# A third normalisation applied after the gate's products instead of before them

## The reference, cut to what matters

```
x = x + mixed @ w_out
x = x + _hier_moe(_rmsnorm(x, ln2), w_rg, b_rg, w_re, b_re, w1, w3, w2)
x = x + jax.nn.sigmoid(_rmsnorm(x, ln3) @ w_ple_gate) * (p @ w_ple_proj)
```

```
def _rmsnorm(x, g):
    y = xf * lax.rsqrt(jnp.mean(xf * xf, axis=-1, keepdims=True) + EPS)
    return (y * g.astype(jnp.float32)).astype(x.dtype)
```

## Time and profile before

| | us |
|---|---|
| median of 3 runs | 1957.49 |
| lowest and highest | 1956.63, 1961.32 |
| the profiled execution, its own time | 1956.76 |
| its span | 1955.0 |
| PE busy | 1816.6 |
| DVE, ACT, POOL busy | 1154.0, 880.4, 118.4 |

### The profile page before, as it was taken

The page is one execution under the profiler, slowest core; times in us unless marked ns, Lnnn a source line. Parts: engine busy times, 40 slices in busy tenths (PEclk is TensorE's granted clock), DMA queues, the critical chain, the costliest instruction groups (busy, mean ns, idle before and its releaser), DMA issues.

```text
span 1955.0 us, 23219 instructions
## 1 busy us (share of the span) xinstructions
PE 1816.6 (93%) x9628; PEld 1526.7 (78%) x9628; DVE 1154.0 (59%) x1373; ACT 880.4 (45%) x982; POOL 118.4 (6%) x75
## 2 busy tenths in 40 slices
PE   5999889747999999999999899999999999996998
PEld 3899768746877778997897777887887788884898
DVE  4985547897862222323442536886886788885533
ACT  3333355344443435321223235775665666663322
POOL 0100004231320010000000000000000000000000
PEclk9999889878999999999999579999999999999999
DMA  7443433322454354473555237997998899995540
GB/s 221 130 130 99 124 86 89 84 86 65 122 173 140 135 175 147 123 276 120 169 151 169 70 119 241 362 367 257 341 341 290 293 335 342 350 320 148 148 114 27
DMA packets 385912, 365.51 MB, mean 187 GB/s; under 512 B 18388, under 2 KB 361476, under 8 KB 383688
## 3 DMA queue, kind: packets, MB, share of 16 engines
q1 hardware_dynamic: 381704, 345.07, 56.7%
q0 software_dynamic: 4096, 18.88, 2.7%
HBM read 353.19 MB, written 10.72 MB: 186 GB/s over the span
## 4 chain that ended last, share of the span: by engine, by line
PE 83%; DVE 11%; ACT 3%; issue 2%; DMA 1%; POOL 0%; DVEq 0%; SPq 0%; ACTq 0%
PE psum L1577 22%; PE psum L770 18%; PE psum L783 9%; PE psum L1564 7%; PE psum L844 6%; PE psum L732 4%; PE psum L1742 2%; PE psum L1505 2%; PE psum L753 2%; PE psum L1764 1%; PE psum L616 1%; PE psum L1739 1%; PE psum L837 1%; DVE weights_low L2095 1%; DVE arena L2239 1%
## 5 line engine op out<-in xcount | busy, mean ns | idle before, releaser
L1001 DVE TENSOR_TENSOR weights_low<-arena,weights_high 128x2048 fp32r<-128x2048 f32 x192 | 439.7, 2292 | 103.1 <-ACT weights_high L870 102.9
L1577 PE MATMUL psum<-input_high,weights_high 128*128 128x320 f32 x1264 | 406.7, 322 | 47.9 <-ACT arena L1886 25.5
L870 ACT ACTIVATE weights_high<-arena 128x2048 fp32r<-128x2048 f32 x192 | 367.6, 1915 | 108.1 <-PE psum L783 58.3
L1577 PE MATMUL psum<-input_low,weights_high 128*128 128x320 f32 x1264 | 396.1, 313 | 0.0
L1577 PE MATMUL psum<-input_high,weights_low 128*128 128x320 f32 x1264 | 395.7, 313 | 0.0
L1577 PEld LDWEIGHTS psum<-input_high,weights_high 128*128 128x128 f32 x1264 | 243.0, 192 | 65.2 <-ACT arena L1886 30.7
L1577 PEld LDWEIGHTS psum<-input_low,weights_high 128*128 128x128 f32 x1264 | 243.5, 193 | 1.1
L1577 PEld LDWEIGHTS psum<-input_high,weights_low 128*128 128x128 f32 x1264 | 242.6, 192 | 0.1
L2095 DVE TENSOR_TENSOR weights_low<-arena,weights_high 128x1024 fp32r<-128x1024 f32 x128 | 150.9, 1221 | 112.3 <-ACT weights_high L1823 112.3
L770 PE MATMUL psum<-weights_high,gathered_high 128*128 128x512 f32 x512 | 213.6, 417 | 0.0
L1823 ACT ACTIVATE weights_high<-arena 128x1024 fp32r<-128x1024 f32 x162 | 162.0, 1051 | 93.6 <-PE psum L1577 64.2
(11 more groups left out here) (312 smaller groups left out, 2385.1 us busy)
## 6 DMA issues: line engine op xcount, KB each, us to landing
arena<-in_w SPq DMA_DIRECT2D x384, 512.0 KB, 5.6
arena<-in_w_in SPq DMA_DIRECT2D x64, 1024.0 KB, 5.6
arena<-in_w_out SPq DMA_DIRECT2D x16, 1024.0 KB, 5.9
arena<-in_w_ple_gate SPq DMA_DIRECT2D x16, 1024.0 KB, 6.2
arena<-in_w_br_rnn SPq DMA_DIRECT2D x8, 1024.0 KB, 5.3
arena<-in_w_br_attn SPq DMA_DIRECT2D x8, 1024.0 KB, 5.2
branch_spill<-arena SPq DMA_DIRECT2D x14, 320.0 KB, 6.6
arena<-branch_spill SPq DMA_DIRECT2D x1, 4480.0 KB, 16.7
```

Source lines behind the costliest of these rows:

```text
L870: nc.scalar.activation(stage[m % STG][0][:], mslots[m % MRING], ACT.Identity).then_inc(s["high"], 1)
L1001: v.tensor_tensor(lo[:], mslots[m % MRING], hi[:].bitcast(F32), ALU.subtract).then_inc(s["split"], 1)
L1577: last = mm(acc[0:m, 0:T], x[:, P * k:P * k + m], y[:], start=(k == 0 and n == 0), stop=(k == KD - 1 and n == 2))
```

## The change

The third norm is no longer applied to the input of the gate's products. The input is XT times ln3, split into high and low part; the products are multiplied by the root of their token afterwards, on DVE, before the sigmoid. In detail:

- The branch for overfull groups comes ahead of the last group's additions on every engine. (If it is taken, the branch makes these additions itself and empties the selection, so that the later ones add nothing.)
- The last 16 additions use five banks (2 to 6). PE makes 8 of them and then follows each further one with the three products of gate chunk 0 for the channel chunk seven behind it. DVE follows addition k with the low part of chunk k - 2 (`input3_low`, one instruction with XT, ln3 and the high part). ACT makes the high part of chunk k straight from XT with ln3 as scale, then its square.
- The squares are added on POOL (`second_pool`), 15 additions of 128x320 into plg's first half; PE sums over the partitions once instead of 16 times. POOL also makes the low part of gate tile 0. ACT may be two squares ahead of POOL.
- ACT no longer waits for `experts_done`. SP waits for it, instead of for the sums, before it issues the projection weights.
- In the loop the projection comes after the gate products of its chunk, with a semaphore of its own. DVE multiplies the products by the root, ACT takes the sigmoid in SBUF, DVE goes on as before.

```diff
                 if g == NG - 1:
-                    pe.wait_ge(main["sc_add"], KD * g + max(d - 3, 0))
-                    to = bank(d % 4, T)
+                    pe.wait_ge(main["sc_add"], LAST + max(d - 4, 0))
+                    to = bank(2 + d % 5, T)
                 else:
...
-            for d in range(KD):
-                add(NG - 1, d)
-            pe.wait_ge(main["sc_add"], KD * NG)
             more = pe.value_load(flags_i[0:1, 0:1], min_val=0, max_val=2)
             with pe.If(more > 0):
+                pe.wait_ge(main["oa"], NG)
+                pe.wait_ge(main["ob"], NG)
+                add_now(extra, 0, (NG - 1) % 2)
                 pe.sem_inc(extra["used"], STG)
                 experts(extra, 0)
                 with pe.If(more > 1):
                     experts(extra, 1)
-
-            for k in range(KD):
-                sum_sq(2, k)
-            pe.wait_ge(proj_in, 16)
 
...
+            def gate_part(j, k):
+
+                if k == 0:
+                    pe.wait_ge(tile_split, 2 * NT + j + 1)
+                    if j >= 2:
+                        pe.wait_ge(ple_sg, 2 * j - 3)
+                if j == 0:
+                    pe.wait_ge(in_split, 2 * KD + k + 1)
+                for n, (x, y) in enumerate(parts3(stage[j % 2], parts_in[k])):
+                    last = mm(bank(j % 2, T), x[:, P * k:P * (k + 1)], y[:],
+                              start=(k == 0 and n == 0), stop=(k == KD - 1 and n == 2))
+                if k == KD - 1:
+                    last.then_inc(ple_g, 1)
+
+            BEHIND = 7
+            for d in range(KD + BEHIND):
+                if d < KD:
+                    add(NG - 1, d)
+                if d >= BEHIND:
+                    gate_part(0, d - BEHIND)
+            pe.wait_ge(ss_mm, 3 * KD - 1)
+            mm(bank(7, T), C("ones"), sq3_sum, start=True, stop=True).then_inc(ss_mm, 1)
             for j in range(KD):
+                if j:
+                    for k in range(KD):
+                        gate_part(j, k)
+                else:
+                    pe.wait_ge(proj_in, 16)
                 if j >= 2:
                     pe.wait_ge(ple_y, j - 1)
                 for k in range(2):
                     last = mm(bank(2 + j % 2, T), proj[:, k, P * j:P * (j + 1)], pT[:, k, :], start=(k == 0),
                               stop=(k == 1))
-                pe.wait_ge(tile_split, 2 * NT + j + 1)
-                for k in range(KD):
-                    if j == 0:
-                        pe.wait_ge(in_split, 2 * KD + k + 1)
-                    for n, (x, y) in enumerate(parts3(stage[j % 2], parts_in[k])):
-                        last = mm(bank(j % 2, T), x[:, P * k:P * (k + 1)], y[:],
-                                  start=(k == 0 and n == 0), stop=(k == KD - 1 and n == 2))
-                last.then_inc(ple_g, 1)
+                last.then_inc(ple_p, 1)
                 if j:
                     back(j - 1)
             back(KD - 1)
...
-            act.wait_ge(experts_done, 1)
             gate_high(0)
-            gate_high(1)
             for k in range(KD):
-                squares(2, k, XT[:, k, :])
-            root(2)
-            for k in range(KD):
-                act.wait_ge(h_ready, 2 * KD + k + 1)
-                input_high(k)
+                if k == 7:
+                    gate_high(1)
+                act.wait_ge(main["sc_add"], LAST + k + 1)
+                nc.scalar.activation(parts_in[k][0][:], XT[:, k, :], ACT.Identity, scale=vec[:, V_LN3 + k:V_LN3 + k + 1]
+                                     ).then_inc(in_high, 1)
+                if k >= 3:
+                    act.wait_ge(ss_mm, 2 * KD + k - 2)
+                nc.scalar.activation(sq2[:, k % 2, :] if k else sq3_sum, XT[:, k, :], ACT.Square).then_inc(sq_ready, 1)
             for j in range(KD):
                 act.wait_ge(ple_g, j + 1)
                 gate_high(j + 2)
-                if j >= 2:
-                    act.wait_ge(ple_y, j - 1)
-                nc.scalar.activation(sq2[:, j % 2, :], bank(j % 2, T), ACT.Sigmoid).then_inc(ple_sg, 1)
+                if j == 0:
+                    root(2)
+                act.wait_ge(ple_sg, 2 * j + 1)
+                nc.scalar.activation(sq2[:, j % 2, :], sq2[:, j % 2, :], ACT.Sigmoid).then_inc(ple_sg, 1)
                 if j % 4 == 0 and j:
                     turn_out(act, j // 4 - 1)
...
-                from_bank = bank(d % 4 if g == NG - 1 else 3, T)
+                from_bank = bank(2 + d % 5 if g == NG - 1 else 3, T)
...
-            for d in range(KD):
-                add(NG - 1, d)
             with dve.If(more > 0):
+                add_now(extra, 0)
+                v.memset(ST[:, (NG - 1) % 2, :], 0.0)
                 low(extra, 0, 0)
...
-            gate_low(0)
+            def input3_low(k):
+
+                dve.wait_ge(in_high, 2 * KD + k + 1)
+                hi, lo = parts_in[k]
+                v.scalar_tensor_tensor(out=lo[:], in0=XT[:, k, :], scalar=vec[:, V_LN3 + k:V_LN3 + k + 1],
+                                       in1=hi[:].bitcast(F32), op0=ALU.mult, op1=ALU.subtract).then_inc(in_split, 1)
+
+            for k in range(KD):
+                add(NG - 1, k)
+                if k >= 2:
+                    input3_low(k - 2)
+            input3_low(KD - 2)
+            input3_low(KD - 1)
             gate_low(1)
-            normalise(2, XT, V_LN3, G, lambda k: input_low(2, k))
+            dve.wait_ge(ss_mm, 3 * KD)
+            link(v.tensor_scalar(rstd[:], bank(7, T), 1.0 / D, EPS, ALU.mult, ALU.add))
+            v.reciprocal(rstd[:], rstd[:]).then_inc(var_ready, 1)
+            gate_low(2)
             for j in range(KD):
-                gate_low(j + 2)
-                dve.wait_ge(ple_sg, j + 1)
+                if j == 0:
+                    dve.wait_ge(rstd_ready, 3)
+                dve.wait_ge(ple_g, j + 1)
+                z = sq2[:, j % 2, :]
+                v.tensor_tensor(z, bank(j % 2, T), rstd[:], ALU.mult).then_inc(ple_sg, 1)
+                if j:
+                    gate_low(j + 2)
+                dve.wait_ge(ple_sg, 2 * j + 2)
+                dve.wait_ge(ple_p, j + 1)
                 if j >= 2:
                     dve.wait_ge(ple_t, j - 1)
                 y = plg[:, j % 2, :]
-                link(v.tensor_tensor(y, bank(2 + j % 2, T), sq2[:, j % 2, :], ALU.mult))
+                link(v.tensor_tensor(y, bank(2 + j % 2, T), z, ALU.mult))
                 v.tensor_tensor(y, y, XT[:, j, :], ALU.add).then_inc(ple_y, 1)
+
+        def second_pool(pool):
+
+            pool.wait_ge(tile_high, 2 * NT + 1)
+            hi, lo = stage[0]
+            nc.gpsimd.tensor_tensor(lo[:], mslots[0], hi[:].bitcast(F32), ALU.subtract).then_inc(tile_split, 1)
+            for k in range(1, KD):
+                pool.wait_ge(sq_ready, 2 * KD + k + 1)
+                if k > 1:
+                    pool.wait_ge(ss_mm, 2 * KD + k - 1)
+                nc.gpsimd.tensor_tensor(sq3_sum, sq3_sum, sq2[:, k % 2, :], ALU.add).then_inc(ss_mm, 1)
 
...
-                    sp.wait_ge(ss_mm, 3 * KD)
+                    sp.wait_ge(experts_done, 1)
                     sp.dma_start(proj, A["w_ple_proj"][0].rearrange("(k p) n -> p k n", p=P)).then_inc(proj_in, 16)
...
+            second_pool(pool)
```

26 lines of the change are left out of this document (16 added, 10 removed).

## The result

The changed kernel takes 1942.66 us, the median of four runs (1940.12 to 1944.83). The kernel before took 1959.4 us beside it (four runs, 1956.63 to 1963.3). The ratio is 0.9913, with a 95% interval of 0.9889 to 0.9936. A second set of five runs gave 1941.66 us and 0.9918 (0.9904 to 0.9931). The forecast was 1943.0 us.

What follows compares the result with a forecast made beforehand. PE was taken to bound the kernel, with only the 49.1 us from 1773.8 to 1822.89 able to shrink. Chunk 1 starts 14.3 us earlier, the tail is 0.5 longer: 1956.8 - 13.8 = 1943.0 us, range 1935 to 1949.

Steps and rivals of the forecast that it cites:

- Two of its own signs: Listed signs of a wrong or right forecast: first additions well after 1777 (wrong); about 1.4 us a chunk (right).
- The start: Behind the experts' last copy: first addition on DVE at 1776.7, PE about 1777.0, ACT's first weight tile at 1777.4.
- The branch moves ahead of the additions: Overfull-group branch runs beside the last PSUM copy from 1773.8; 2.8 to 2.9 us on DVE, up to 4 more possible.
- The tile: GpSimd makes gate tile 0's low part in about 4.75 us, 1779.35 to 1784.1; DVE's low part 0 waits for it.
- The rival without a collision: DVE's low parts don't collide with GpSimd; ACT paces, chunk 1 at 1801.7, 6.9 us better, 1936 us; 15%.
- The addition: Each of GpSimd's 15 additions of squares, 128x320, takes 0.9 us, within 0.75 to 2.4.
- the pace: DVE low parts of 0.46 us and GpSimd additions of 0.9 alternate, 1.36 us a chunk; last low part at 1805.3.
- Tile 1's low part: DVE's gate_low(1) comes last, 2.26 us, ending at 1807.6; 0.9 more if GpSimd gets one more addition in between.
- Clock: PE may be at 1.2 GHz at 1807, before chunk 1; between 0 and 2.6 us, taken as 1.
- Projection weights: Issued when DVE passes the branch, about 1777, they land before 1790; the old 7.43 us wait on PE is gone.
- Deferred root: Reciprocal and root lie beside chunk 1's products, done at 1812.5, needed at 1817; cost nothing, 4 us of cover.
- Tail: At the kernel's end, the last chunk's new multiplication by the root on DVE has no cover and adds 0.5 us.

## Why the prediction was right, step by step

**The time.** 1943.0 us was right to 0.3 us. The order and the waits were as forecast, but the third of a microsecond is luck, and more than the working deserves. Its saving, 13.8 us, was 3 us too small by the medians; it was taken from 1956.8, a low execution of the kernel before, whose median came out at 1959.4. And inside the saving two errors of 3 to 5 us stood against each other. Two of its own signs spoke against it: the first additions came well after 1777 (DVE's at 1785.58), and a chunk took 1.085 us, not about 1.4.

**The start (too cheap).** The step "The branch moves ahead of the additions" took DVE's 2.8 us as the nearest row, with DVE's first addition at +2.9 and GpSimd's tile at +5.6. They came at +8.0 and +8.6. What failed was the choice of engine and state: the row showed DVE with empty queues, and PE and ACT, which did show no branch of their own, lost 5.4 and 5.6 us with the tiles in flight. The text had up to 4 us more in the range; it belonged in the sum. It also had DVE's first addition at 1776.7, ahead of the product of PE that it needs, at 1777.0; before, the two stood 0.8 us apart. That was off the path, which went over GpSimd's tile.

**The tile (right).** 4.52 us for 4.75, and low 0 held until it ended, as forecast, with the gap on DVE between the third and fourth addition. The rival without a collision fell here.

**The addition (right) and the pace (too dear).** 0.938 us for 0.9; the 0.95 worked out from the Trainium skill (GPSIMD Engine Reference, "Performance versus the Vector engine") was nearer still. But 0.46 + 0.9 = 1.36 a chunk became 1.085, because a duration was used as if all of it excluded the other engine. Over fifteen chunks that is 4.1 us. From the tile's end to the last low part it was 16.5 us for 21.2. The right reading would have been GpSimd's chain alone, an addition and the step to the next, 1.00 us, and a little for the meeting.

**Tile 1's low part.** Taken at 2.26, measured 2.95, the 0.7 us more being the meeting with GpSimd's last addition; the prediction spoke of 0.9. **Clock.** 1 us, 0 here, 0.9 to 1.4 in the kernels in which it fell. **Projection weights.** No wait, as forecast. The sum was right not to count the 7.43 us as gain, since it found chunk 1 by the new order; as a lone edit they are worth nothing, which the first part of the prediction didn't say.

**Deferred root.** No cost: DVE scales chunk 0's products at 1814.70 and chunk 2's products start at 1818.82, in the period of 8.45. **Tail.** From the last gate product to the end it is 6.8 us before and 7.3 now, 0.6 us more for 0.5. The other 0.3 of the 0.8 is chunk 1's start from rest.

**Sum.** Chunk 1 was expected 34.8 us behind +0 and came at 32.5: 2.8 us later by the tile's end, 4.7 earlier by the pace, 0.6 later by tile 1, 1 earlier by the clock.

## What to carry to other kernels

A long wait on the chain of the last-ended work isn't its own worth: look which engine is busy under it, because removing the wait can shorten the time only down to what that engine needs. A branch in a stretch with heavy transfers cost PE up to twice what it cost in a quiet one (8.0 and 3.8 us), so hold back transfers that aren't yet needed, or place it where PE has other work and the queues are empty. Between DVE and GpSimd count the collision by what the shorter engine leaves free, not by the sum of durations, and never let a long tile instruction of one meet a short, waited-for instruction of the other.

## What the runs showed of the hardware

- Stepping over the branch with the queues empty: 1.71 us on DVE, 2.97 on ACT, 3.81 on PE. With weight tiles in flight, at about 290 GB/s when the branch came: gaps of 2.8 to 5.6 on ACT, and on PE 4.9 to 8.0 beyond the 1.36 us of the copy, in one or two pieces.
- PE's gap ended 1.3 to 1.7 us after a 16 KB instruction packet had landed, in 11 profiles of 11. The packet took 0.9 to 1.5 us with or without the tiles in flight; with them it started later.
- The exclusion of DVE and GpSimd goes both ways and hits whole tiles: a 0.87 us addition of GpSimd took 2.68 and 2.73 us beside DVE's two-input 128x2048, and a 0.55 us low part of DVE 4.15 us beside GpSimd's. Two short ones of 0.55 and 0.87 us, alternating, took 0.76 and 0.94 us.
- PE's grant at the end of the stage differed between profiles with the same busy share ahead of it. Where it fell, the stretch behind the last low part was 0.9 to 1.4 us longer. What decides that stays open. So does why PE's gap is one piece in some profiles and two in others.
